# VectorE takes two thirds of the full exponential tiles into its own sums, the first weights come in parts, and head 0's preparation is reordered

## The reference, cut to what matters

```python
sc = (jnp.einsum('bqhd,bkhd->bhqk', qn, k_nope)
      + jnp.einsum('bqhr,bkr->bhqk', qr, k_rope)).astype(jnp.float32) * scale
mask = key_chunk[None, :] <= q_chunk[:, None]
sc = jnp.where(mask[None, None], sc, NEG_INF)
p = jax.nn.softmax(sc, axis=-1).astype(v.dtype)
return jnp.einsum('bhqk,bkhd->bqhd', p, v)
```

## Time and profile before

| | |
|---|---|
| median of 3 runs | 1630.59 us |
| the profiled execution, slowest core | 1631.05 us |
| its span, first to last instruction | 1629.2 us |
| TensorE busy | 1579.5 us (97%) |
| VectorE busy | 1073.2 us (66%) |
| ScalarE busy | 626.9 us (38%) |
| spans of the 8 cores | 1626.6 to 1629.2 us |
| start to first matmul | 18.8 us |
| attention, first to last step | 783.2 to 1088.6 us |

### The profile page before, as it was taken

One profiled execution on the slowest core, in us unless ns is written; L12 is line 12 of the kernel. 1 busy time (PEld: TensorE's weight loads), 2 busy tenths in 40 slices (PEclk: granted clock), 3 DMA queues, 4 the chain that ended last, 5 costly groups with the idle time before them and its releaser, 6 DMA issues.

```text
span 1629.2 us, 22883 instructions; the slowest of 8 cores (1626.6 to 1629.2 us)
## 1 busy us (share of the span) xinstructions
PE 1579.5 (97%) x7640; PEld 728.6 (45%) x7640; DVE 1073.2 (66%) x1714; ACT 626.9 (38%) x1107; POOL 84.6 (5%) x110
## 2 busy tenths in 40 slices
PE   4999999999999999999899999999999999999996
PEld 1444444444444444444454545444444444444442
DVE  3678867777779977674533333316877777777777
ACT  3621134322222222456566666663432222222243
POOL 0000000212100000000000000000000000000000
PEclk9999999999999999999999999999999999999998
DMA  8721404232223231103100000050421313131105
GB/s 172 169 40 30 72 16 65 40 72 40 39 34 58 35 50 17 23 1 47 27 9 1 8 1 1 5 88 1 65 40 27 52 27 52 27 51 28 27 1 207
DMA packets 29234, 71.79 MB, mean 44 GB/s; under 512 B 1792, under 2 KB 3072, under 8 KB 28224
## 3 DMA queue, kind: packets, MB, share of 16 engines
q0 software_dynamic: 24960, 47.39, 18.7%
q1 hardware_dynamic: 4160, 22.94, 4.3%
HBM read 107.48 MB, written 8.39 MB: 71 GB/s over the span
## 4 chain that ended last, share of the span: by engine, by line
PE 94%; DVE 2%; DMA 2%; ACT 1%; issue 1%; DVEq 0%; ACTq 0%; SPq 0%; POOLq 0%
PE ps L303 76%; PE ps L1048 4%; PE ps L1050 3%; PE ps L1021 3%; PE ps L1020 3%; PE ps L330 2%; DMA sb_W<-w_in 1%; PE ps L964 1%; PE ps L481 1%; DVE sb_h L350 1%; DMA sb_E<-sb_W 0%; DVE sb_sq L977 0%; ACT sb_sq L321 0%; ACT sb_E L1042 0%; ACT sb_sq L1056 0%
## 5 line engine op out<-in xcount | busy, mean ns | idle before, releaser
L303 PE MATMUL ps<-sb_A,sb_W 128*128 128x512 bf16 x3856 | 858.4, 379 | 0.0
L303 PEld LDWEIGHTS ps<-sb_A,sb_W 128*128 128x128 bf16 x3856 | 377.2, 98 | 454.8 <-issue 0.3
L303 PE MATMUL ps<-sb_B,sb_W 128*128 128x512 bf16 x1664 | 387.5, 379 | 0.0
L367 DVE TENSOR_TENSOR sb_h<-ps,sb_h 128x512 f32<-128x512 f32 x384 | 259.9, 688 | 64.2 <-PE ps L303 61.5
L644 DVE SCALAR_TENSOR_TENSOR sb_E<-sb_Dg,sb_cst,sb_E 128x512 f32<-128x512 f32 x352 | 264.8, 752 | 37.2 <-DVE sb_E L640 0.5
L649 ACT ACTIVATE sb_E<-sb_E,sb_cst 128x512 f32<-128x512 f32 x176 | 127.2, 723 | 330.6 <-DVE sb_E L644 330.4
L303 PEld LDWEIGHTS ps<-sb_B,sb_W 128*128 128x128 bf16 x1664 | 162.8, 98 | 196.3
L634 ACT COPY sb_Dg<-ps 128x512 f32<-128x512 f32 x176 | 103.0, 585 | 257.2 <-PE ps L303 257.2
L640 DVE TENSOR_SCALAR sb_E<-sb_Dg,sb_cst 128x512 f32<-128x512 f32 x176 | 86.9, 494 | 141.1 <-ACT sb_Dg L634 140.4
L936 DVE CAST sb_B<-ps 128x512 bf16<-128x512 f32 x90 | 62.2, 691 | 122.3 <-PE ps L303 61.5
L321 ACT ACTIVATE sb_sq<-sb_h 128x1024 bf16<-128x1024 f32 x80 | 84.1, 1052 | 119.9 <-DVE sb_h L367 97.1
(11 more groups left out here) (97 smaller groups left out, 823.9 us busy)
## 6 DMA issues: line engine op xcount, KB each, us to landing
sb_W<-w_up POOLq DMA_DIRECT2D x44, 512.0 KB, 6.4
sb_W<-w_down POOLq DMA_DIRECT2D x10, 1024.0 KB, 11.3
sb_W<-w_in POOLq DMA_DIRECT2D x8, 768.0 KB, 9.7
outT<-sb_h SPq DMA_DIRECT2D x3, 2048.0 KB, 7.2
sb_h<-xT SPq DMA_DIRECT2D x8, 512.0 KB, 11.5
sb_h<-xT SPq DMA_DIRECT2D x2, 2048.0 KB, 12.2
sb_W<-w_out POOLq DMA_DIRECT2D x1, 2048.0 KB, 16.2
sb_W<-w_o POOLq DMA_DIRECT2D x8, 256.0 KB, 10.1
```

What stands on the lines that cost most here:

```text
L303: ins = e.matmul(banks[bank][:, :], l, r, start=(i == 0), stop=(i == n - 1))
L367: add("dve", lambda e: e.tensor_tensor(out=hv.ap, in0=banks[bank][:, :], in1=hv.ap, op=ALU.add), r=[PS[bank], hv], w=[hv])
```

## The change

```diff
-            win(0)
-            win(1, [H(4, 0, 2)])
+            def win_part(j, i, n, after=()):
+                sz = 3072 // n
+                off = (0, 6 * K)[slot_of[j]] + i * sz * 2
+                part_ = W2.at(off, sz)
+                add("pool", lambda e: e.dma_start(out=part_.ap, in_=win_d[j, :, i * sz:(i + 1) * sz],
+                                                  max_dma_last_dim=4096), r=after, w=[part_], dma="wp%d%d" % (j, i))
+                return part_
             for q4 in range(4):
-                sdma(H(2 * q4, 1, 2), xT_d[1, ...], "x1_%d" % q4, r=[H(6, 0, 2)])
-            win(2, [H(2, 1, 2)])
-            win(3, [H(6, 1, 2)])
+                win_part(0, q4, 4)
+            w1a = win_part(1, 0, 2, [H(4, 0, 2)])
+            win_part(1, 1, 2, [H(6, 0, 2)])
+            for q4 in range(4):
+                sdma(H(2 * q4, 1, 2), xT_d[1, ...], "x1_%d" % q4, r=[w1a])
+            win(2, [H(4, 1, 2)])
+            win(3, [slots[2]])
...
                 if paced:
                     for k in range(8):
+                        for f in fill.get(k, ()):
+                            f()
+                        wk = View(slot.ap, slot.res[k * 768 // 512:((k + 1) * 768 + 511) // 512])
...
-                                r=[slot, arr[k]], w=[PS[bank]])
-                        for f in fill.get(k, ()):
-                            f()
+                                r=[wk, arr[k]], w=[PS[bank]])
+                    for f in fill.get(8, ()):
+                        f()
...
             unit(0, 0, rawfill(0, "dve"), paced=True)
-            unit(1, 0)
-            feed(1, 0, "act")
-            feed(1, 1, "act")
             drain_tail()
+            unit(1, 0, [lambda: (feed(1, 0, "act"), feed(1, 1, "act"))])
+            drain_tail()
             unit(0, 1, rawfill(1, "act"), paced=True)
...
-            for j, (b0, n) in enumerate(((0, TT), (TT, 3 * TT))):
+            for j, (b0, n) in enumerate(((0, 2 * TT), (2 * TT, 2 * TT))):
...
+            ring = [E.at(i * K, TT) for i in (0, 1, 2, 9)]
+            accs = [(W4.at(9 * K, TT, F32), W4.at(11 * K, TT)), (B.at(0, TT, F32), B.at(2 * K, TT))]
+            acc_lo = E.at(18 * K, TT)
+            held = []
...
-                        out.append(lambda f=f, tt=tt: f(hd, tt, pool, eng if f is not p_v else "dve"))
+                        out.append(lambda f=f, tt=tt: f(hd, tt, pool, eng if f is not p_v or tt % 2 == 0 else "dve"))
...
-                    p = pt(pt_cnt[0] % 3)
+                    p = ring[pt_cnt[0] % 4]
...
-                add("pe", lambda e: e.matmul(banks[lb][:, c0:TT], ones, p.ap[:, c0:TT], start=first, stop=last),
-                    r=[ONE, p], w=[PS[lb]])
+                split = qt >= 2
+                acc, acc_hi = accs[hd == NHEAD - 1]
+                if split and d < 0 and kb % 3 != 2:
+                    if kb == 0:
+                        held.append(p)
+                    else:
+                        q_ = held.pop() if held else acc
+                        add("dve", lambda e: e.tensor_tensor(out=acc.ap, in0=p.ap, in1=q_.ap, op=ALU.add),
+                            r=[p, q_], w=[acc])
+                else:
+                    begin = kb == (2 if split else 0)
+                    add("pe", lambda e: e.matmul(banks[lb][:, c0:TT], ones, p.ap[:, c0:TT], start=begin,
+                                                 stop=last and not split), r=[ONE, p], w=[PS[lb]])
+                if last and split:
+                    add("dve", lambda e: e.tensor_copy(out=acc_hi.ap, in_=acc.ap), r=[acc], w=[acc_hi])
+                    add("dve", lambda e: e.tensor_tensor(out=acc_lo.ap, in0=acc.ap, in1=acc_hi.ap, op=ALU.subtract),
+                        r=[acc, acc_hi], w=[acc_lo])
+                def rest_of_l():
+                    for v, fin_ in ((acc_hi, False), (acc_lo, True)):
+                        add("pe", lambda e, v=v, fin_=fin_: e.matmul(banks[lb][:, :], ones, v.ap, start=False,
+                                                                     stop=fin_), r=[ONE, v], w=[PS[lb]])
...
-                    todo.extend([None, ln, None, inv])
+                    todo.extend([None, rest_of_l, ln, inv] if split else [None, ln, None, inv])
...
-            head = t01[:5] + r01[:1] + t01[5:] + r01[1:3] + t2_[:2] + r01[3:] + t2_[2:]
+            head = t01[:2] + r01[:2] + t01[2:] + t2_[:1] + r01[2:3] + t2_[1:2] + r01[3:] + t2_[2:]
+            later, lat = [f for x in lat[2:3] + lat[4:] for f in x], lat[:2] + lat[3:4]
...
-            early, late = head_pieces(0, (3,), mb_) + rope_pieces(0, (2, 3), mb_), []
+            early, late = rope_pieces(0, (2,), mb_) + later + rope_pieces(0, (3,), mb_) + head_pieces(0, (3,), mb_), []
...
-                if k < 10:
-                    while n_early and n_early - len(early) < (k + 1) * n_early / 9 and early:
+                ew = 22 if hd == 0 else 10
+                if k < ew:
+                    while n_early and n_early - len(early) < (k + 1) * n_early / (ew - 1) and early:
...
-                    lim = (k + 1) * n_late / 37 if not n_early else (k - 9) * n_late / 28
+                    lim = (k + 1) * n_late / 37 if not n_early else (k + 1 - ew) * n_late / (38 - ew)
```

More of the change, by code:

```diff
@@ L430, in xin @@
                 sdma(H(0, tt, 8), xT_d[tt], "x%d" % tt, r=after)
-            win(0)
-            win(1, [H(4, 0, 2)])
-            for q4 in range(4):
-                sdma(H(2 * q4, 1, 2), xT_d[1, :, q4 * 1024:(q4 + 1) * 1024], "x1_%d" % q4, r=[H(6, 0, 2)])
-            win(2, [H(2, 1, 2)])
-            win(3, [H(6, 1, 2)])
+            def win_part(j, i, n, after=()):
[5 more added lines that the diff above has]
+                return part_
+            for q4 in range(4):
+                win_part(0, q4, 4)
+            w1a = win_part(1, 0, 2, [H(4, 0, 2)])
+            win_part(1, 1, 2, [H(6, 0, 2)])
+            for q4 in range(4):
+                sdma(H(2 * q4, 1, 2), xT_d[1, :, q4 * 1024:(q4 + 1) * 1024], "x1_%d" % q4, r=[w1a])
+            win(2, [H(4, 1, 2)])
+            win(3, [slots[2]])
             xin(2, [slots[2]])
@@ L545, in rawfill @@
                 return {2: [mm, lambda: feed(tt, 2, eng)], 4: [mm, lambda: feed(tt, 3, eng)], 6: [mm],
-                        7: [mm, lambda: fin2(norms[tt], tt)]}
+                        8: [mm, lambda: fin2(norms[tt], tt)]}
             feed(0, 0, "dve")
@@ L1088, in mla @@
                     n_early, n_late = len(early), len(late)
[L1089 to L1092, removed]
+                if hd == NHEAD - 1 and k == 5:
+                    for oc in range(8):
+                        wdma(wout_panel(oc), wo_d[oc], "wo%d" % oc)
+                    up_prefetch(1)
                 sbk = sq_.pop(0)
```

## The result

| | before | changed |
|---|---|---|
| median | 1630.76 us | 1613.38 us |
| ratio, 95% interval | | 0.9893 (0.9875 to 0.991) |
| span of the slowest core | 1629.2 us | 1611.2 us |
| first step of the attention | 783.24 us | 774.43 us |
| first matmul of the projection behind it | 1088.4 us | 1071.0 us |

The changed kernel is 17.4 us faster; 19.2 were forecast.

A forecast was written before the change was run, and what follows sets the result against it. TensorE, busy 97% of the span, was taken as the bound. Attention -8.8, head 0 0, before the attention -3.9 and the start -6.5 summed to -19.2 us, a median of 1611.4 us, range 1603 to 1621.

The forecast's parts named there:

- The ones-products, -17.3: Attention: net 80 matmuls fewer on TensorE at 0.216 us each, -17.3 us if TensorE stays the bound.
- (a): Attention, step 24: ones-products wait for cast and difference behind a filler's copy on VectorE, +4.3 us (0 to 7).
- (b): End of query tiles: `ln` waits for the two extra ones-products, 0.4 us a head, +3.2 us (0 to 7).
- (c): Last head, no fillers: ScalarE sets the pace in diagonal steps, half of its 2.2 us saving lost, +1.0 us (0 to 2).
- Head 0, 0 (-2 to +3): Head 0's own steps: about -1.5 us from spreading early fillers, +2 from dense late ones, taken as 0.
- Fillers share one bank ... Nothing there: Attention: a filler's copy behind one sum ends 1.55 us after the last matmul, two steps lie between fillers; no cost.
- the wait for bank 7: Attention: sign of a wrong prediction, TensorE waiting at fillers for their one PSUM bank; no size given for the sign.
- Before the attention, -3.9: Preparation before the attention: first tables land earlier, first step at 779.3 instead of 783.2, -3.9 us (-5 to -1.5).
- The start, -6.5: Start: first weights loaded in parts and feeds earlier, -6.9 us, less 0.4 for block 3: -6.5 us (-9 to 0).
- rival 2: The start gives nothing: TensorE stays at 1.2 GHz through unit (1,0), +5.2 us, block 3 late; 1617.7 us; chance 0.14.
- The ring of four buffers: Attention: exponential buffers are asked for again at least 2.6 us on, against sums 0.7 us behind; later reads covered.
- rival 3: Attention: 112 places with a VectorE sum ahead of a copy or product wait 0.1 us more, +8.8, 1620.2 us; chance 0.10.

The follow-up runs named there:

- e10: The changed kernel with no filler in steps 22 and 23 of heads 1 to 7; ratio 0.9852 to the kernel before.
- e6: The changed kernel with cast and difference issued early and their two ones-products in the last diagonal step; attention 297.2 us on core 0, 296.8 with the early cast alone.
- e3: The kernel before with only the preparation's part, including the new spread of head 0's fillers, no sums on VectorE; ratio 0.9989 (0.9976 to 1.0002).
- e4: The kernel before with VectorE's sums, casts and differences added but used by nobody, all ones-products kept on TensorE; ratio 0.9994 (0.9984 to 1.0003).
- e8: The changed kernel with head 0's early filler list over 14 steps instead of 22; head 0 took 42.36 us on core 1, against 42.34.
- e7: The changed kernel with 16 unread matmuls between units (0,0) and (1,0); spans on cores 0 to 3 1607.5 to 1609.6 us, against 1609.0 to 1611.0.
- e12: The changed kernel with steps 22 and 23 filler-free, 16 unread matmuls at the start, head 0's early list over 14 steps, last head's cast and products earlier; 1607.7 us.
- e1: The kernel before with the attention's part alone: sums on VectorE, four buffers, two extra ones-products, w_o loaded at step 5; 1619.8 us, ratio 0.9934.

## Why the prediction was right

- **The ones-products, -17.3.** Right: 37.30 in an odd head where I said 37.2 for a middle one, and VectorE at 23.8 us there (25 said). A mixed sum lasted 0.68 us (0.69 taken), the cast 0.42 (0.48), the difference 0.69.
- **(a) +4.3.** Right in place and price: 1.26 us ahead of L1086 in three heads and 0.61 in head 2 is 4.4, plus 0.25 in head 0 (1.0 said), and `e10` gave 4.5 back in heads 1 to 5. What I had not seen is that the cast can't be saved by issuing it earlier.
- **(b) +3.2.** Mis-sized: 0.75 us, all in the last head (`e6`). Outside it the loss ahead of the product with V is nearly the same as before (0.52 to 0.68 against 0.53 us in odd heads, 0.98 to 1.15 against 1.05 in heads 2, 4 and 6). I worked the step out with no filler; that fillers, or the old wait for ScalarE, cover it in the other heads is argued and not shown.
- **(c) +1.0.** About half: the last head's length less its matmuls at 0.216 us was 3.6 us where it was 2.3, so 1.3, of which 0.75 is (b)'s.
- **Head 0, 0 (-2 to +3).** The failed step. "Spread over 22 steps these stop waiting" came true where the pieces had stood: tile 1 lost 0.25 us between matmuls instead of 2.5. But tile 3 lost 4.3 us instead of nothing (2.8 in `e3`, without any sums), tile 0 1.1 more and tile 2 0.7. In all head 0 lost 7.0 us instead of 3.2, and only 0.25 of it is (a)'s: the term is +3.5. Nearly all of it lies before fillers, 6.1 us instead of 2.7. So the step "Fillers share one bank ... Nothing there" is wrong in head 0, and the wait for bank 7, which the prediction names as a sign of being wrong, appeared.
- **Before the attention, -3.9.** Right: -4.0 (8.81 for the first step less 4.84 for the start), and -4.0 alone.
- **The start, -6.5.** Mis-sized: -4.84. First matmul at 11.5 instead of 10, block 1 at 25.8 as forecast (25.5), and then rival 2's mechanism in part: 7.03 us instead of 5.3 for unit (1,0), 1.7 us. Unit (0,1) ran 6.9 us at TensorE's own pace. The matmuls 0.43 us apart in unit (1,0), a second sign of being wrong, were there for part of it. The forecast took a core; the time is that of the slowest, and the landing of block 1 differed by over 2 us between cores.

Sum: -4.8 - 4.0 - 8.6 = -17.4, and -0.6 behind the attention, is the span's 18.0. Within the attention the terms are -17.3, (a) +4.6, (b) and (c) together +1.3, head 0 +3.5, and a gain that I had not named, 0.9 us less lost in heads 1 to 6 outside (a), mostly before fillers. Head 0's error of 3.5 us was cancelled by (b)'s 2.5, (c)'s 0.4 and this 0.9: that the attention's total came within 0.2 us of -8.8 is luck. What is left is the start's 1.7.

Two smaller steps did not hold. The ring of four buffers does not cover the sums' later reads: exponentials on ScalarE waited for a sum 12 times, 3.7 us in all, which cost TensorE little here. And rival 3's sum is off: 112 places at 0.1 us are 11.2 us and not 8.8.

The rule of the Trainium skill, DMA: Bandwidth & Descriptors, section on bandwidth, against cutting up loads, did not decide here: the last of block 0's four parts landed at 18.5 us, where the whole block was there at 18.8, and the block was used up by 20.5. What came late was block 1, asked for behind it. The other rule, in the Trainium skill's TensorE: Matmul & The Clock Gate, Part 1, that idling brings the half rate, agrees in kind: unit (1,0) after 3.9 us of idling, with 24 matmuls in 7.89 us, is a fall. I had written that no row showed one, having read one core; core 2 of the same trace has it at the attention's first matmuls (granted clock 0.50).

## What to carry to other kernels

When work is moved from a saturated engine to one with room, count the matmuls and then look at the queue at the few places where the new results are read: there a helper's copy ahead of them cost 4.5 us here, while the moved operations by themselves cost none in `e4`. Move the helper, not the result; an engine that is only half busy is still the wrong place for a copy when its next instruction is one that the critical engine needs. And a filler list that is stretched in one place is dense in another; if the waits belong to the list and not to the place, the total stays, as in `e8`. Last, read the clock on every core, behind each wait of TensorE and not only at the start.

## What was not expected of the hardware

- After a wait for weights, TensorE came back at the fast or at the slow level with little relation to the length of the wait: 24 matmuls took 5.34 us after 3.18 and 3.55 us of idling on two cores with the start alone, and 7.03 after 2.60 on core 5 of the changed kernel. Sixteen matmuls in the wait made it 5.34 on cores 0 to 3 of `e7` and on all eight of `e12`.
- The clock also fell in the middle of a run. In `e1`, after waits of 2.1 and 2.6 us with six matmuls between, cores 1, 5 and 7 began the attention at a granted clock of 0.50, and core 3, with the same two waits, at 1.00; it was worth 1.2 us of head 0.
- The second block of weights landed at 23.4 to 25.8 us by core in one execution of the changed kernel, with the same program on each.
- A float32 to bf16 cast within SBUF took 0.42 us, and a float32 sum with one bf16 operand 0.68, the same as with two float32 ones.
